# Feed-forward of a two-layer encoder: the down-projection tiles of a chunk placed in threes between the last three groups of the next chunk's up projection

## The reference, cut to what matters

```
def conv_ffn(x, conv_prev, w_up, conv_w, conv_b, w_down):
    u = x @ w_up                          # 1024 -> 2 * 2816
    ue = jnp.concatenate([conv_prev, u], 1)
    c = conv_b
    for j in range(CONV_W):               # 3 taps, causal
        c = c + ue[:, j:j + T] * conv_w[j]
    a, b = jnp.split(c, 2, axis=-1)
    y = (jax.nn.silu(a) * b) @ w_down     # 2816 -> 1024
    return y, ue[:, -(CONV_W - 1):]
```

## Time and profile before

| | |
|---|---|
| median of three runs | 3266.03 us |
| the profiled execution | 3263.73 us |
| its span, first to last instruction | 3261.9 us |
| mean granted TensorE clock, share of full | 0.968 |
| PE busy / DVE / ACT / POOL | 93% / 50% / 31% / 25% |
| feed-forward loops of the two layers | about 945 to 1650 us and 2433 to 3138 us |
| one chunk (up and down) in these | 38.38 us, 38 times |

### The profile page before, as it was taken

How to read it: one execution, slowest core, us unless ns; L and a number is a source line. 1 busy time by engine, 2 the same in 40 slices (tenths; PEclk the granted TensorE clock), 3 DMA queues, 4 the chain that set the end, 5 groups by cost and what they waited for, 6 DMA issues and landing times. The chain is left out here.

```text
span 3261.9 us, 41395 instructions
## 1 busy us (share of the span) xinstructions
PE 3040.5 (93%) x15759; PEld 2593.9 (80%) x15759; DVE 1633.5 (50%) x2252; ACT 1009.5 (31%) x1921; POOL 808.5 (25%) x685
## 2 busy tenths in 40 slices
PE   8799789996999999999995998997999999999996
PEld 6455467775799888999984897885889999998894
DVE  3466224565444555554547442444545445555547
ACT  4344121222332322232233453333332322222232
POOL 1245011112232222233323100101132333223233
PEclk9999899998999999999997998998999999999998
DMA  2100431103111111111111101113111111111111
GB/s 104 35 7 7 154 119 27 40 21 117 48 46 45 39 45 39 39 39 40 44 32 69 58 11 38 37 33 108 39 57 39 39 40 44 45 39 40 44 33 70
DMA packets 71877, 160.45 MB, mean 49 GB/s; under 512 B 19194, under 2 KB 33675, under 8 KB 70708
## 3 DMA queue, kind: packets, MB, share of 16 engines
q1 hardware_dynamic: 70612, 150.51, 14.7%
q0 software_dynamic: 1152, 8.39, 0.7%
HBM read 144.42 MB, written 15.11 MB: 49 GB/s over the span
## 5 line engine op out<-in xcount | busy, mean ns | idle before, releaser
L124 PE MATMUL psum<-xT_hi,tk_whi 128*128 128x384 f32 x2112 | 712.5, 337 | 2.7 <-POOL tk_wlo L1825 1.5
L125 PE MATMUL psum<-xT_lo,tk_whi 128*128 128x384 f32 x2112 | 711.7, 337 | 0.0
L126 PE MATMUL psum<-xT_hi,tk_wlo 128*128 128x384 f32 x2112 | 711.6, 337 | 0.0
L2175 DVE TENSOR_TENSOR x_or_mix<-x_or_mix,psum 128x1024 f32<-128x1024 f32 x342 | 417.9, 1222 | 331.1 <-PE psum L126 330.8
L124 PEld LDWEIGHTS psum<-xT_hi,tk_whi 128*128 128x128 f32 x2112 | 396.7, 188 | 6.0 <-ACT tk_u L2039 4.0
L125 PEld LDWEIGHTS psum<-xT_lo,tk_whi 128*128 128x128 f32 x2112 | 396.6, 188 | 1.8
L126 PEld LDWEIGHTS psum<-xT_hi,tk_wlo 128*128 128x128 f32 x2112 | 396.5, 188 | 0.0
L2160 DVE SCALAR_TENSOR_TENSOR tk_c<-tk_u,tk_cw,tk_c 128x1168 f32<-128x1168 f32 x88 | 126.5, 1438 | 423.9 <-ACT tk_c L2047 423.9
L124 PE MATMUL psum<-tk_dhi,tk_gh 128*128 128x512 f32 x756 | 317.8, 420 | 10.4 <-DVE x_or_mix L2180 8.8
L125 PE MATMUL psum<-tk_dlo,tk_gh 128*128 128x512 f32 x756 | 299.2, 396 | 0.0
L126 PE MATMUL psum<-tk_dhi,tk_gl 128*128 128x512 f32 x756 | 297.4, 393 | 0.0
(11 more groups left out here) (361 smaller groups left out, 5245.3 us busy)
## 6 DMA issues: line engine op xcount, KB each, us to landing
tk_wraw<-in_w_up SPq DMA_DIRECT2D x88, 512.0 KB, 3.6
tk_draw<-in_w_down SPq DMA_DIRECT2D x44, 512.0 KB, 3.6
x_or_mix<-in_c_ckvT SPq DMA_DIRECT2D x8, 1024.0 KB, 5.6
s_ckv<-in_c_ckv POOLq DMA_DIRECT2D x8, 1024.0 KB, 5.1
retw_raw<-in_w_ret SPq DMA_DIRECT2D x32, 256.0 KB, 3.6
tk_mix_wraw<-in_w_out SPq DMA_DIRECT2D x16, 512.0 KB, 4.8
glaw_raw<-in_w_gla SPq DMA_DIRECT2D x32, 192.0 KB, 3.3
x_or_mix<-in_xT SPq DMA_DIRECT2D x9, 512.0 KB, 9.9
```

What stands on the lines that cost most here:

```text
L124: nc.tensor.matmul(out, a[0], b[0], start=first, stop=False)
L125: nc.tensor.matmul(out, a[0], b[1], start=False, stop=False)
L126: return nc.tensor.matmul(out, a[1], b[0], start=False, stop=last)
L2175: nc.vector.tensor_tensor(XM[:, t, :], XM[:, t, :], flat(b, b + 2), ALU.add).then_inc(ad, 1)
```

## The change

`down` takes the tiles it is to do, and waits for the gate and the down weights at its first tile alone. `up` takes an optional pair (chunk, parity): after each of the three groups of branch 1 it does three of that chunk's down tiles. So the order on PE goes from "6 groups, 9 tiles" to "4 groups, 3 tiles, 1 group, 3 tiles, 1 group, 3 tiles", for the same 38 pairs of chunks. The programs of the other engines, the tile order and all semaphore counts stay as they are.

```
-            def up(j):
+            def up(j, between=None):
                 for ab in range(2):
                     pe.wait_ge(us, 2 * j + ab + 1)
                     for q in range(3):
                         pe.wait_ge(ur, 6 * j + 3 * ab + q - 2)
                         up_part(ab, q)
+                        if between and ab:
+                            down(*between, range(3 * q, 3 * q + 3))
...
-            def down(j, par):
-                pe.wait_ge(gs, j + 1)
-                pe.wait_ge(dsp, j + 1)
-                for t in range(NT):
+            def down(j, par, tiles):
+                if tiles[0] == 0:
+                    pe.wait_ge(gs, j + 1)
+                    pe.wait_ge(dsp, j + 1)
+                for t in tiles:
                     ge(pe, ad, 9 * j + max(t - 1, 0) + 1)
...
             with pe.Fori(0, (NJ - 4) // 2) as r:
-                up(2 * r + 1)
-                down(2 * r, 0)
-                up(2 * r + 2)
-                down(2 * r + 1, 1)
-            up(LAST - 2)
-            down(LAST - 3, 0)
+                up(2 * r + 1, (2 * r, 0))
+                up(2 * r + 2, (2 * r + 1, 1))
+            up(LAST - 2, (LAST - 3, 0))
             up(LAST - 1)
             up(LAST)
```

## The result

The changed kernel takes 3321.97 us (median of 4 runs, 3311.14 to 3323.77) against 3266.38 for the kernel before (4 runs): ratio 1.0166, 95% interval 1.0142 to 1.019. It is slower by 1.7%; the forecast was 3324. The profiled execution took 3320.49 us, 56.8 more than the profiled one of the kernel before; the sum had said 58.

What follows compares the result with a forecast made beforehand. PE was taken to bound the kernel, busy in every microsecond of both loops, so only stalls between its matmuls count. Stalls of 2.43 us for 0.90 per chunk, times 38, add 58 us to 3266.03: 3324 us, range 3310 to 3358.

Steps and rivals of the forecast that it cites:

- the sum: PE's stalls per chunk: 2.43 us in place of 0.90, so +1.53 us, times 38 chunks +58 us.
- Part 1: PE's down tiles: one 0.22 us stall in each three, three for four per chunk, gaining 0.24 us per chunk, 9 us.
- the hold-up: On DVE, the second tap of conv(j, 0) takes 3.35 us in place of 1.44 beside POOL's subtraction.
- Part 2: First three: DVE's conv(j, 0) precedes the adds, the first add is 1.77 us late, PE's third tile stalls 1.99 us.
- Part 4: First down tile, now wanted at T + 4.19, T being branch 1's first matmul: gate ready 6.9 us before, no cost.
- Part 5: PE's four more switches per chunk between 384- and 512-column groups: taken as 0, upper bound 17 us.
- the clock rival: PE's new wait of about 1.9 us also lowers its clock: 3356 us if half the 38 waits, 3388 if all; chance 0.16.
- The faster rival: POOL's subtraction comes behind DVE's second tap, which takes 1.44 us; only 9 us gained, 3257 us; chance 0.06.

Runs made afterwards that it cites:

- the kernel with adds first: The changed kernel with DVE's adds of tiles 0 to 2 put before conv(j, 0): 3256.72 us, ratio 0.9978 to the kernel before.
- the pieces with the old order: The changed kernel with down tiles in pieces of 2, 2, 2 and 3, conv(j, 0) still ahead of all nine adds: 3310.93 us, ratio 1.0147.

## Why the prediction was right

*Part 1, one stall per three:* right. 114 short waits, three per chunk, and the pieces without the hold-up take 4.34 to 4.36 where 4.11 + 0.22 = 4.33 was said.

*Part 2, the convolution in front of the first add:* right in mechanism and size. The add was put between 1.73 and 1.81 us late; it came 3.31 - 1.58 = 1.73 late, the lower bound, because the add starts a little ahead of the modelled end of the tap. The first three lost 1.96 us, which is its third tile's stall, where 1.99 was said. That it is this meeting was shown from three sides: shorten the tap, move the pieces, or reorder DVE, and the loss goes each time; with the kernel before, the same shortening gives nothing.

*Part 4, the gate wanted earlier:* no wait on it shows, as said: the gate's lo part is ready 6.9 us before the first down tile in the changed kernel (1131.27 against 1138.20, for one chunk), the margin that was worked out. *Part 5, switching:* nothing, as taken; the bound of 17 us was far too wide, since the kernel with adds first has all four switches and is 7 us faster than the kernel before.

*The sum:* 39.91 us per chunk forecast, 39.92 measured in the chunk shown. 38 x 1.54 = 58.5 us against 56.8 between the two profiled executions and 55.6 between the medians. The 2 to 3 us between them are the base of the sum: it took every chunk of the kernel before to be 38.38 us, where the mean was 38.45.

The Trainium skill's exclusive lock (SBUF — State Buffer, section "SBUF: two separate sides") would have had the tap end 1.44 us behind POOL's subtraction, by the prediction's estimate 8 us more in all; it ended 1.23 behind. The order of events agrees with it: once POOL's subtraction comes after the tap, the tap takes 1.44 us. And the subtraction's own 2.83 us are in line with the same rule turned round, since it started while the first tap was running; where it did not, it took 2.40.

*The rivals:* the clock rival did not happen in the changed kernel (PEclk 1.00 in both loops) but was nearer than its chance of 0.16 lets one think: with the wait longer by 0.32 us it happened in 16 of 38 chunks, at about the price that had been worked out (1.68 forecast, 1.6 measured). That the wait came out at 1.61 us and not near the 1.93 that brings falls was not foreseen: the prediction called it about 1.9, so on the clock it was in part lucky. The faster rival needed POOL to start behind the tap; made true by hand, it gave its side of the answer, though 4 us by the timed runs and not 9 (9.7 in the profiled loops).

## What to carry to other kernels

Before work is moved earlier on the bounding engine, look at what its consumer does at the new time, in program order: here DVE had all the idle time that was needed, but a convolution stood in front of the adds in its program. Tiles that go through two sets of banks wait for nobody in pieces of two, provided the consumer is free in time; so when the producer's work is moved, the consumer's instructions are to be moved with it. And a wait that recurs on TensorE has a second price once it grows long enough for the clock to fall: check the granted clock, not the wait alone.

## What the runs showed of the hardware

- Waits of PE of 1.6 to 1.7 us, one in each chunk of 39.7 to 39.9 us, left the granted clock at 1.00 in every loop (the changed kernel, and the pieces with the old order). Waits of 1.9 us brought it down to the level of 1.2 GHz behind 16 of 38, for some 3.5 us where a timeline was read, and waits of 2.2 us behind 13 of 38. A wait longer by 0.3 us cost 35 us in 38 chunks and not 12.
- A DVE operation on two SBUF tensors (1.44 us alone) that starts while POOL subtracts ends 1.23 to 1.24 us behind the subtraction, whether it started 0.71 us into it (3.35 us long) or 0.62 (3.02 us long, the subtraction being the shorter one of 2.40). The subtraction takes 2.83 us if it starts 0.57 us before the end of such a DVE operation, and about 2.40 beside an add or alone.
- A DVE add with one input in PSUM keeps its 1.22 us beside the same subtraction, and the subtraction its 2.40.
